# RWKV operands in three DRAM arrays instead of one, in an encoder layer

## The chip, the cores and the metric

The kernel runs on one core of a Trainium2 chip. The time is the device time of one execution in microseconds (us); three runs of the kernel before are given by their median. The core has five engines with an instruction stream each: PE (TensorE, matrix products; its weight loads appear as PEld), DVE (VectorE), ACT (ScalarE), POOL (GpSimd) and SP (SyncE, which here only issues DMA transfers). They meet through semaphores alone. The on-chip memory has 128 partitions, called lanes here.

## The reference, cut to what matters

One encoder layer over 1280 tokens (a prompt of 256 and a sample of 1024): a SwiGLU block, two token mixers side by side (gated linear attention and RWKV-7), cross-attention into 256 memory tokens, and a second SwiGLU block. The change touches the RWKV-7 mixer alone: 8 heads of 64 features, run once forward and once backward in time.

```python
def _rwkv7_scan(r, decay, k, v, kk, a, reverse):
    def step(S, inp):
        r_t, w_t, k_t, v_t, kk_t, a_t = inp
        sa = jnp.einsum('bhij,bhj->bhi', S, -kk_t)
        S = (S * w_t[:, :, None, :] + sa[..., None] * (kk_t * a_t)[:, :, None, :]
             + v_t[..., None] * k_t[:, :, None, :])
        y = jnp.einsum('bhij,bhj->bhi', S, r_t)
        return S, y
...
y = (_rwkv7_scan(rH, dec_f, k2, vH, kk, aH, reverse=False)
     + _rwkv7_scan(rH, dec_b, k2, vH, kk, aH, reverse=True))
```

## The kernel before

The layer is computed in phases that follow one another; each ends when all engines have arrived and the phase's transfers have landed. The two that matter are `rwkv_prepare_phase` and, right behind it, `rwkv_scan_phase`. What passes between them is an array in DRAM, `pack`.

**The preparation** works on four tiles (t = 0 to 3) of 128 lanes by 1280 tokens; a tile holds two heads, lanes 0 to 63 the even one (e = 0) and lanes 64 to 127 the odd one (e = 1). It fills an on-chip tile `rwp_pack` of 128 lanes x 20 chunks x 450 columns: v, r, two runs of accumulated log decay (65 columns for each direction, called g), k, kk and b. ACT copies r (L1200) and v (L1203), DVE writes g (L1258, L1260), k (L1269), kk (L1280) and b (L1282). SP stores the tile in two transfers: first v, r and g (L1126, "store A", semaphore `stored_a`), and when b is there k, kk and b (L1128, "store B", `stored_b`). There is one `rwp_pack` for all four tiles, so in the next tile ACT waits for `stored_a` ahead of its copies, and DVE for `stored_a` ahead of g and for `stored_b` ahead of k. SP's queue is in program order; between the stores stand the loads of the next tile's inputs (L1107), of small weights (L1122), and the stores of gate (L1119) and bonus (L1130). At the phase's end SP waits for every store (L1132).

**The scan** takes 20 steps, one for each chunk of 64 tokens and, at the same time, the backward direction's chunk. It is software-pipelined by hand: a step carries four chunks n, n+1, n+2, n+3 in different stages. For chunk c SP issues eight loads of operands into `rws_pack` (L1379: for each direction and each e two pieces) and eight of v into `rws_hv` and `rws_uv` (L1365); both tiles have two buffers. The loads of chunk c wait until the work of chunk c-2 has read its buffer. ACT's exponentials (L1620, L1621) and POOL's scalings (L1404, L1407, L1417) wait for `loaded`; PE waits for `v_loaded` ahead of `right_side`. A load's DRAM side is made of runs of 64, 129, 192 or 257 floats (256 to 1028 bytes), one for each lane and tile, 256 of them in a transfer.

Of the kernel before, what the change touches and what calls it, by code (L numbers as in the profile page):

```python
# [20 lines left out]
P = 128  # L21
# [13 lines left out]
C = 64  # L35
# [14 lines left out]
V_COL, R_COL, G_COL = 0, C, 2 * C  # L50
K_COL = G_COL + 2 * (C + 1)
KK_COL, B_COL, PACK = K_COL + C, K_COL + 2 * C, K_COL + 3 * C
# [1010 lines left out]
def rwkv_prepare_phase(nc, a, proj_d, pack_d, vecs, bonus_d, gate_d, consts):  # L1063
# [5 lines left out]
    with ExitStack() as ctx:  # L1069
# [13 lines left out]
        stored_a, stored_b, gate_stored, bonus_stored = (m.sem(n) for n in ("stored_a", "stored_b", "gate_stored", "bonus_stored"))  # L1083
        coef, low_scaled, low_ready = m.sem("coef"), m.sem("low_scaled"), m.sem("low_ready")
# [14 lines left out]
        @block.sync  # L1099
        def _(sp):  # L1100
            for j, tile in enumerate((DECAY_TILE, LOW_TILE, GATE_TILE)):
                sp.dma_start(raw2[:, 1, j], proj_d[tile]).then_inc(small_in, 16)
            sp.dma_start(lora[:], a["lora"][0]).then_inc(lora_in, 16)

            def load(t):
                for j, tile in enumerate((R_TILE, KR_TILE, VR_TILE)):
                    sp.dma_start(raw2[:, t % 2, j], proj_d[tile + t]).then_inc(loaded[t % 2], 16)  # L1107

            load(0)
            sp.dma_start(keep[:], a["keep"]).then_inc(keep_in, 16)  # L1110
# [20 lines left out]
            for sem in (stored_a, stored_b, gate_stored, bonus_stored):  # L1131
                sp.wait_ge(sem, 64)  # L1132
# [40 lines left out]
        def _(act):  # L1173
# [7 lines left out]
            for t in range(4):  # L1181
# [32 lines left out]
        def _(dve):  # L1214
            nc.vector.tensor_tensor(stay[:], vecs[:, MU_PREV:MU_PREV + MU_TILES], vecs[:, MU_NEXT:MU_NEXT + MU_TILES], ALU.add).then_inc(coef, 1)
# [19 lines left out]
            for t in range(4):  # L1235
# [8 lines left out]
                for d in range(2):  # L1244
# [7 lines left out]
                    if t:  # L1252
                        dve.wait_ge(stored_a, 16 * t)
                    end = C - 1 if d == 0 else 0
                    first = G_COL + d * (C + 1)
# [11 lines left out]
                if t:  # L1267
                    dve.wait_ge(stored_b, 16 * t)
# [22 lines left out]
def rwkv_scan_phase(nc, pack_d, out, consts):  # L1291
# [8 lines left out]
    with ExitStack() as ctx:  # L1300
# [3 lines left out]
        G_AT, K_AT = C, 2 * C + 2  # L1304
        KK_AT, B_AT, PACKED = K_AT + C, K_AT + 2 * C, K_AT + 3 * C
        pack = slots("pack", [P, 8, PACKED], 2)
# [79 lines left out]
        def _(pool):  # L1386
            for u in range(2):
                nc.gpsimd.memset(pack[u][own(0), :, G_AT + C + 1:G_AT + C + 2], 0.0).then_inc(ready, 1)
                nc.gpsimd.memset(pack[u][own(1), :, G_AT:G_AT + 1], 0.0).then_inc(ready, 1)
            pool.wait_ge(ready, 4)  # L1390
# [3 lines left out]
            pool.wait_ge(ready, 8)  # L1394

            def scale(c):
                packed = lambda at, lanes=slice(0, P): pack[c % 2][lanes, :, at:at + C]
                pool.wait_ge(loaded[c % 2], 128 * (c // 2 + 1))
# [38 lines left out]
        def _(pe):  # L1437
            pe.wait_ge(ready, 8)
# [76 lines left out]
            def step(n, m, p, s):  # L1515
                state, inverting, preparing = n is not None, m is not None, p is not None

                if state:
# [3 lines left out]
                    pe.wait_ge(v_loaded[n % 2], 128 * (n // 2 + 1))  # L1522
# [86 lines left out]
        def _(act):  # L1609
            act.wait_ge(ready, 4)  # L1610

            def exponentials(c):
                act.wait_ge(loaded[c % 2], 128 * (c // 2 + 1))
# [435 lines left out]
def mix_phases(nc, a, proj_d, gla_d, v_d, decay, pack_d, side_d, vecs, mix_o, mix_y, mem, mem_in):  # L2049

    with ExitStack() as mixing:
# [4 lines left out]
        rwkv_prepare_phase(nc, a, proj_d, pack_d, vecs, side_d[0], side_d[1], consts)  # L2056
        rwkv_scan_phase(nc, pack_d, mix_y, consts)
# [3 lines left out]
def build(nc, a, out_d):  # L2061
# [4 lines left out]
    pack_d = nc.dram_tensor("pack", (N_CHUNKS, P, 4, PACK), F32, kind="Internal").ap()  # L2066
# [152 lines left out]
```

## Time and profile before

| | |
|---|---|
| median of 3 runs | 4101.01 us (4097.25 to 4107.3) |
| the profiled execution | 4109.71 us, span 4107.9 us |
| mean granted TensorE clock | 0.942 of full |
| PE, DVE, ACT, POOL busy | 88%, 43%, 26%, 7% of the span |
| preparation (1611 to 1795 us of the span) | 184 us |
| scan (1795 to about 2300 us) | 505 us |

The span runs from the first to the last instruction of one execution; 1.8 us of that execution lie outside. Busy shares are averages over phases with different limits, so the two phases have to be read by themselves.

### The profile page before, as it was taken

The numbers are of one execution on the slowest core, as the hardware profiler recorded it, in microseconds if no ns is written. First come the engines' busy times: TensorE is split into PE (matmuls) and PEld (weight loads), VectorE is DVE, ScalarE is ACT, GpSimd is POOL, SyncE is SP. The second block draws the span as 40 slices with busy tenths as digits, with TensorE's granted clock in tenths as the row PEclk, the third lists the DMA queues.
The fourth block names the chain that finished last, engine by engine and source line by source line (L and its number), as shares of the span: only waits on it lengthen the run. The fifth ranks groups of instructions, "written<-read, shape, count | busy, mean of one in ns | idle before, by whom it ended". The sixth has DMA issues, their size and how long they took to land. (4 is left out here: it accounts for less than half of the span.)

```text
span 4107.9 us, 71757 instructions
## 1 busy us (share of the span) xinstructions
PE 3601.8 (88%) x30856; PEld 3026.3 (74%) x30856; DVE 1753.1 (43%) x2247; ACT 1053.5 (26%) x1355; POOL 303.0 (7%) x295
## 2 busy tenths in 40 slices
PE   7999999997999974548888688797897999999997
PEld 5888888885888873227777466686786888888885
DVE  4545454446121144744444432502235445454445
ACT  2111111104232224435555331312223111111103
POOL 0000000000010010034544100000000000000000
PEclk9999999998999967769999899998999999999998
DMA  2101001000333243663433232001101101011001
GB/s 109 46 31 46 31 32 45 31 21 11 116 123 103 98 127 127 194 147 79 84 78 66 88 105 100 10 31 42 36 21 41 46 31 46 31 39 38 31 21 51
DMA packets 182674, 261.85 MB, mean 64 GB/s; under 512 B 62528, under 2 KB 144832, under 8 KB 176192
## 3 DMA queue, kind: packets, MB, share of 16 engines
q1 hardware_dynamic: 172240, 239.46, 19.3%
q10 hardware_dynamic: 10224, 19.27, 1.2%
q8 instruction: 171, 2.80, 0.3%
q14 instruction: 39, 0.32, 0.0%
HBM read 194.77 MB, written 63.91 MB: 63 GB/s over the span
## 5 line engine op out<-in xcount | busy, mean ns | idle before, releaser
L294 DVE TENSOR_TENSOR main_acc<-main_acc,ffn_psum 128x512 f32<-128x512 f32 (+1 forms) x1056 | 617.5, 598 | 853.8 <-PE ffn_psum L217 852.8
L206 PE MATMUL ffn_psum<-x_xh,ffn_wi_h 128*128 128x512 f32 (+1 forms) x2112 | 525.1, 357 | 49.2 <-DVE ffn_wi_l L283 49.2
L206 PE MATMUL ffn_psum<-x_xh,ffn_wi_l 128*128 128x512 f32 (+1 forms) x2112 | 525.1, 357 | 0.0
L206 PE MATMUL ffn_psum<-x_xl,ffn_wi_h 128*128 128x512 f32 (+1 forms) x2112 | 525.0, 357 | 0.0
L206 PEld LDWEIGHTS ffn_psum<-x_xh,ffn_wi_h 128*128 128x128 f32 x2112 | 372.6, 188 | 117.1 <-DVE ffn_wi_l L283 49.6
L206 PEld LDWEIGHTS ffn_psum<-x_xh,ffn_wi_l 128*128 128x128 f32 x2112 | 349.9, 188 | 60.6
L206 PEld LDWEIGHTS ffn_psum<-x_xl,ffn_wi_h 128*128 128x128 f32 x2112 | 349.3, 188 | 61.1
L217 PE MATMUL ffn_psum<-ffn_hid_h,ffn_wo_h 128*128 128x512 f32 (+1 forms) x1056 | 380.5, 360 | 12.7 <-DVE ffn_hid_l L302 10.0
L217 PE MATMUL ffn_psum<-ffn_hid_h,ffn_wo_l 128*128 128x512 f32 (+1 forms) x1056 | 377.7, 358 | 0.0
L217 PE MATMUL ffn_psum<-ffn_hid_l,ffn_wo_h 128*128 128x512 f32 (+1 forms) x1056 | 376.5, 357 | 0.0
L258 ACT CAST ffn_hid_h<-ffn_hid 128x1280 fp32r<-128x1280 f32 x44 | 55.6, 1264 | 1090.3 <-DVE ffn_hid L300 1090.3
L217 PEld LDWEIGHTS ffn_psum<-ffn_hid_h,ffn_wo_h 128*128 128x128 f32 x1056 | 198.9, 188 | 62.6 <-DVE main_acc L294 12.0
L217 PEld LDWEIGHTS ffn_psum<-ffn_hid_h,ffn_wo_l 128*128 128x128 f32 x1056 | 198.9, 188 | 31.6
L217 PEld LDWEIGHTS ffn_psum<-ffn_hid_l,ffn_wo_h 128*128 128x128 f32 x1056 | 199.3, 189 | 16.7
L677 PE MATMUL mixin_psum<-x_xh,mixin_w_h 128*128 128x512 f32 (+1 forms) x648 | 167.4, 367 | 16.5 <-DVE mixin_w_l L778 16.5
L254 ACT ACTIVATE ffn_hid<-ffn_psum 128x1280 f32<-128x1280 f32 x44 | 54.7, 1243 | 495.2 <-PE ffn_psum L206 495.2
L677 PE MATMUL mixin_psum<-x_xl,mixin_w_h 128*128 128x512 f32 (+1 forms) x648 | 162.5, 359 | 0.0
L677 PE MATMUL mixin_psum<-x_xh,mixin_w_l 128*128 128x512 f32 (+1 forms) x648 | 162.3, 359 | 0.0
L778 DVE TENSOR_TENSOR mixin_w_l<-mixin_w_raw,mixin_w_h 128x1024 fp32r<-128x1024 f32 x27 | 34.5, 1281 | 267.4 <-ACT mixin_w_h L693 267.4
L1441 PE MATMUL rws_psum<-rws_x,rws_gb 64*64 64x64 f32 x3200 | 119.1, 222 | 33.6 <-ACT rws_x L1659 27.7
L1441 PEld LDWEIGHTS rws_psum<-rws_x,rws_gb 64*64 64x64 f32 x3200 | 104.2, 135 | 50.0 <-ACT rws_x L1659 37.7
L677 PEld LDWEIGHTS mixin_psum<-x_xh,mixin_w_h 128*128 128x128 f32 x648 | 109.0, 189 | 39.1 <-DVE mixin_w_l L778 16.9
(279 smaller groups left out, 5391.1 us busy)
## 6 DMA issues: line engine op xcount, KB each, us to landing
ffn_w_raw_in<-ffn_w_in_dram SPq DMA_DIRECT2D x44, 1024.0 KB, 6.3
ffn_w_raw_out<-ffn_w_out_dram SPq DMA_DIRECT2D x44, 512.0 KB, 3.5
mixin_w_raw<-mix_w_in_dram SPq DMA_DIRECT2D x27, 512.0 KB, 3.5
proj<-mixin_stage ACTq DMA_DIRECT2D x18, 640.0 KB, 3.0
pack<-rwp_pack SPq DMA_DIRECT2D x4, 2580.0 KB, 10.7
rws_pack<-pack SPq DMA_DIRECT2D x40, 257.0 KB, 4.5
gla<-main_acc SPq DMA_DIRECT2D x4, 2560.0 KB, 10.1
glas_now<-gla SPq DMA_DIRECT2D x40, 256.0 KB, 3.0
```

Source lines behind the costliest of these rows:

```text
L206: mm = nc.tensor.matmul(ps[:, at + c * BANK:at + c * BANK + tn], w[:, slot, cols], x[:, k, t0:t0 + tn], start=(k == 0 and j == 0), stop=(k ...
L217: mm = nc.tensor.matmul(ps[:, at:at + tn], w[:, slot, o * P:(o + 1) * P], h[:, t0:t0 + tn], start=(j == 0), stop=(j == 2))
L254: nc.scalar.activation(hid[:], ps[:, gate_at:gate_at + T], ACT.Silu).then_inc(silu_done, 1)
L258: nc.scalar.copy(hid_h[:], hid[:]).then_inc(hid_high, 1)
L294: nc.vector.tensor_tensor(acc[:, o, t0:t0 + tn], acc[:, o, t0:t0 + tn], ps[:, at:at + tn], ALU.add).then_inc(added, 1)
L677: mm = nc.tensor.matmul(ps[:, at:at + tn], w[:, u, k * P:(k + 1) * P], x[:, k, t0:t0 + tn], start=(k == 0 and j == 0), stop=(k == KT - 1 a ...
L778: nc.vector.tensor_tensor(w_l[:, u, :], raw[:, u, :], w_h[:, u, :], ALU.subtract).then_inc(split, 1)
L1441: return nc.tensor.matmul(dst, lhs, rhs_, start=start, stop=stop, skip_group_check=True)
```

## The change

The one array becomes three, laid out as the scan reads them: `shared` (r, k, kk, b; chunk, lane, tile, e, 256 columns), `grow` (g, one part for each direction, 66 columns with a zero column that the scan's POOL used to set) and `rwkv_v`. A lane of a chunk is now one run of 8192, 2112 or 2048 bytes, and a load has 64 of them. The scan issues eight transfers a step for sixteen. The preparation's columns are put in another order, and its stores go by halves of the lanes, since the array's rows have 64 lanes: store A is six transfers (v: runs of 256 bytes; g: runs of 264 bytes), store B two (r, k, kk, b: runs of 1024 bytes). As r moves from store A to store B, ACT's copy of r waits for `stored_b` of the tile before instead of `stored_a`.

```diff
@@ rwkv_prepare_phase, SP
-                sp.wait_ge(copied, t + 1)
+                sp.wait_ge(edge_set, 1)
                 sp.wait_ge(v_set, 3 * (t + 1))
                 sp.wait_ge(centred, 4 * (t + 1))
-                sp.dma_start(pack_d[:, :, t, 0:K_COL].rearrange("c p w -> p c w"), pack[:, :, 0:K_COL]).then_inc(stored_a, 16)
+                for e in range(2):
+                    lanes = slice(e * C, (e + 1) * C)
+                    sp.dma_start(v_d[:, :, t, e].rearrange("c l w -> l c w"), pack[lanes, :, V_COL:V_COL + C]).then_inc(stored_a, 16)
+                    for d, (g0, g1) in enumerate(G_ENDS):
+                        sp.dma_start(g_d[d, :, :, t, e].rearrange("c l w -> l c w"), pack[lanes, :, g0:g1]).then_inc(stored_a, 16)
+                sp.wait_ge(copied, t + 1)
                 sp.wait_ge(b_packed, t + 1)
-                sp.dma_start(pack_d[:, :, t, K_COL:PACK].rearrange("c p w -> p c w"), pack[:, :, K_COL:PACK]).then_inc(stored_b, 16)
+                for e in range(2):
+                    lanes = slice(e * C, (e + 1) * C)
+                    sp.dma_start(shared_d[:, :, t, e].rearrange("c l w -> l c w"), pack[lanes, :, R_COL:PACK]).then_inc(stored_b, 16)
@@ rwkv_prepare_phase, ACT
                 if t:
-                    act.wait_ge(stored_a, 16 * t)
+                    act.wait_ge(stored_b, 32 * t)
                 nc.scalar.copy(part(R_COL), view(r[:])).then_inc(copied, 1)
+                if t:
+                    act.wait_ge(stored_a, 96 * t)
@@ rwkv_prepare_phase, DVE
+            nc.vector.memset(pack[:, :, G_COL + C + 1:G_COL + C + 2], 0.0).then_inc(edge_set, 1)
@@ rwkv_scan_phase, SP
                 for d in DIRS:
-                    for e in range(2):
-                        for tile in (hv, uv):
-                            sp.dma_start(tile[c % 2][other(d), d].rearrange("p (q e) t -> p q e t", e=2)[:, :, e],
-                                         pack_d[chunk_of(c)[d]][LANES[e], :, V_COL:V_COL + C]).then_inc(v_loaded[c % 2], 16)
+                    for tile in (hv, uv):
+                        sp.dma_start(tile[c % 2][other(d), d], v_d[chunk_of(c)[d]].rearrange("l q e w -> l (q e) w")).then_inc(v_loaded[c % 2], 16)
...
                 for d in DIRS:
-                    chunk = pack_d[chunk_of(c)[d]]
-                    ends = ((R_COL, G_COL + C + 1), (K_COL, PACK)) if d == 0 else ((R_COL, R_COL + C), (G_COL + C + 1, PACK))
-                    for e in range(2):
-                        dst = pack[c % 2][own(d)].rearrange("p (q e) w -> p q e w", e=2)[:, :, e]
-                        for (s0, s1), at in zip(ends, (0, K_AT if d == 0 else G_AT + 1)):
-                            sp.dma_start(dst[:, :, at:at + s1 - s0], chunk[LANES[e], :, s0:s1]).then_inc(loaded[c % 2], 16)
+                    sp.dma_start(g[c % 2][own(d)], g_d[d, chunk_of(c)[d]].rearrange("l q e w -> l (q e) w")).then_inc(loaded[c % 2], 16)
+                    sp.dma_start(pack[c % 2][own(d)], shared_d[chunk_of(c)[d]].rearrange("l q e w -> l (q e) w")).then_inc(loaded[c % 2], 16)
@@ rwkv_scan_phase, POOL
-            for u in range(2):
-                nc.gpsimd.memset(pack[u][own(0), :, G_AT + C + 1:G_AT + C + 2], 0.0).then_inc(ready, 1)
-                nc.gpsimd.memset(pack[u][own(1), :, G_AT:G_AT + 1], 0.0).then_inc(ready, 1)
-            pool.wait_ge(ready, 4)
```

On SP's queue, one tile of the preparation read as follows before; the shapes are lanes x chunks x columns, and `rwp_pack` is the on-chip tile.

```order
L1126 DMA pack<-rwp_pack 128x20x258 [waits rwp_centred,rwp_v_set,rwp_copied]
L1128 DMA pack<-rwp_pack 128x20x192 [waits rwp_b_packed]
L1130 DMA side<-rwp_bonus 128x1280 [waits rwp_kept]
L1107 DMA rwp_raw<-proj 128x1280 [waits rwp_b_packed]
L1107 DMA rwp_raw<-proj 128x1280 x2
```

It now reads as follows (line numbers are those of the changed file).

```order
L1130 DMA rwkv_v<-rwp_pack 64x20x64 [waits rwp_centred,rwp_v_set,rwp_edge_set]
L1132 DMA grow<-rwp_pack 64x20x66 x2
L1130 DMA rwkv_v<-rwp_pack 64x20x64
L1132 DMA grow<-rwp_pack 64x20x66 x2
L1137 DMA shared<-rwp_pack 64x20x256 [waits rwp_b_packed,rwp_copied]
L1137 DMA shared<-rwp_pack 64x20x256
L1139 DMA side<-rwp_bonus 128x1280 [waits rwp_kept]
```

Two transfers became eight, none moved past another kind; the wait for r's copy stands ahead of store B now.

On SP's queue, the loads of one chunk and one chunk's v in the scan were these.

```order
L1379 DMA rws_pack<-pack 64x4x129 [waits rws_ar_set,rws_bk_set,rws_exps]
L1379 DMA rws_pack<-pack 64x4x192
L1379 DMA rws_pack<-pack 64x4x129
L1379 DMA rws_pack<-pack 64x4x192
L1379 DMA rws_pack<-pack 64x4x64
L1379 DMA rws_pack<-pack 64x4x257
L1379 DMA rws_pack<-pack 64x4x64
L1379 DMA rws_pack<-pack 64x4x257
L1365 DMA rws_hv<-pack 64x4x64
L1365 DMA rws_uv<-pack 64x4x64
```

They are now these.

```order
L1383 DMA rws_g<-grow 64x528 [waits rws_ar_set,rws_bk_set,rws_exps]
L1384 DMA rws_pack<-shared 64x2048
L1383 DMA rws_g<-grow 64x528
L1384 DMA rws_pack<-shared 64x2048
L1375 DMA rws_hv<-rwkv_v 64x512
L1375 DMA rws_uv<-rwkv_v 64x512
```

The order of the loads, and what they wait for, is as it was; each covers 64 lanes before and after.

## Rows read from the trace of the kernel before

**Rows 1.** the page: the span; a DMA queue with its packets, MB, share of 16 engines.

```profile
span 4107.9 us, 71757 instructions
...
q8 instruction: 171, 2.80, 0.3%
```

**Rows 2.** windows: preparation, scan; busy us per engine, PEclk, DMA share, GB/s.

```profile
1611.00:1795.00 184.00, 91.61 (x464) 45.60 (x464) 127.46 (x119) 83.04 (x73) 0.11 (x1) 0.69 0.64 192
...
1854.00:2206.00 352.00, 301.52 (x10572) 268.16 (x10576) 160.70 (x285) 189.02 (x361) 176.14 (x165) 1.00 0.40 79
```

**Rows 3.** who waited for whom, PE, in the scan (1794 to 2300).

```profile
PE rws_psum L1441 <- ACT rws_x L1659: 27.7, 42, 0.7
PE rws_psum L1441 <- issue: 23.6, 32, 2.0
```

**Rows 4.** the same for ACT, then its timeline where that wait ends.

```profile
ACT rws_grown L1620 <- DMA rws_pack<-pack: 24.4, 1, 24.4
...
1804.11 0.65 ACT L1620 ACTIVATE rws_grown<-rws_pack 128x528 f32<-128x528 f32 x1 [24.44 <-DMA rws_pack<-pack]
```

**Rows 5.** timeline of SP's queue: first and last tile of the preparation, scan start.

```profile
1654.66 0.37 SPq L1126 DMA_DIRECT2D pack<-rwp_pack  x1
1669.84 0.37 SPq L1128 DMA_DIRECT2D pack<-rwp_pack  x1
...
1673.50 3.82 SPq L1107 DMA_DIRECT2D rwp_raw<-proj  x3
...
1767.57 0.37 SPq L1126 DMA_DIRECT2D pack<-rwp_pack  x1
1782.75 0.37 SPq L1128 DMA_DIRECT2D pack<-rwp_pack  x1
1784.44 1.77 SPq L1130 DMA_DIRECT2D side<-rwp_bonus  x1
1794.84 1.18 SPq L1379 DMA_DIRECT2D rws_pack<-pack  x2
```

**Rows 6.** waits of SP's queue, end of the preparation.

```profile
SPq L1132 <- DMA side<-rwp_bonus: 5.9, 1, 5.9
```

**Rows 7.** windows of single transfers; the last two columns are DMA share and GB/s.

```profile
1227.00:1231.00 4.00, 4.00 (x23) 3.38 (x22) 0.00 (x0) 0.00 (x0) 0.00 (x0) 1.00 1.04 347
...
1656.00:1660.00 4.00, 3.29 (x4) 1.52 (x5) 1.70 (x2) 1.94 (x2) 0.00 (x0) 0.50 1.04 349
1784.00:1788.00 4.00, 0.00 (x0) 0.00 (x0) 0.41 (x1) 0.00 (x0) 0.00 (x0) 0.69 1.01 325
...
1800.00:1804.00 4.00, 0.00 (x0) 0.00 (x0) 1.27 (x3) 0.00 (x0) 0.00 (x0) 0.50 1.11 204
...
1836.00:1838.00 2.00, 2.00 (x65) 1.78 (x68) 1.42 (x3) 0.52 (x1) 1.27 (x2) 0.82 1.17 151
```

**Rows 8.** timeline of ACT in the second tile, idle time before in brackets.

```profile
1683.82 1.27 ACT L1200 COPY rwp_pack<-rwp_r 128x1280 f32<-128x1280 f32 x1
...
1692.86 1.27 ACT L1206 ACTIVATE rwp_decay<-rwp_kk 128x1280 f32<-128x1280 f32 x1 [6.14 <-DVE rwp_kk L1261]
```

**Rows 9.** timeline of DVE in the same stretch.

```profile
1685.90 1.49 DVE L1258 SCALAR_TENSOR_TENSOR rwp_pack<-rwp_raw 128x1280 f32<-128x1280 f32 x1
...
1693.72 1.49 DVE L1269 TENSOR_TENSOR rwp_pack<-rwp_kr,rwp_raw 128x1280 f32<-128x1280 f32 x1
```

**Rows 10.** DMA issues by line: count, KB each, median us to landing.

```profile
pack<-rwp_pack SPq DMA_DIRECT2D x4, 2580.0 KB, 10.7
...
rwp_raw<-proj SPq DMA_DIRECT2D x15, 640.0 KB, 8.6
...
pack<-rwp_pack SPq DMA_DIRECT2D x4, 1920.0 KB, 12.2
```

**Rows 11.** waits of PE: scan with loads, then its last 83 us.

```profile
PE rws_psum L1441 <- issue: 20.1, 26, 2.0
...
PE rws_psum L1441 <- issue: 1.9, 4, 0.7
```

More of the change, by code:

```diff
@@ L48 @@
 DECAY_UNIT = float(np.exp(-0.5))
-V_COL, R_COL, G_COL = 0, C, 2 * C
-K_COL = G_COL + 2 * (C + 1)
-KK_COL, B_COL, PACK = K_COL + C, K_COL + 2 * C, K_COL + 3 * C
+V_COL, G_COL = 0, C
+R_COL = G_COL + 2 * (C + 1) + 1
+K_COL, KK_COL, B_COL, PACK = R_COL + C, R_COL + 2 * C, R_COL + 3 * C, R_COL + 4 * C
+G_ENDS = ((G_COL, G_COL + C + 2), (G_COL + C + 1, R_COL))
 MEM_T = 512
@@ L1122, in _ @@
                     sp.dma_start(lora[:], a["lora"][t + 1]).then_inc(lora_in, 16)
-                sp.wait_ge(copied, t + 1)
+                sp.wait_ge(edge_set, 1)
                 sp.wait_ge(v_set, 3 * (t + 1))
                 sp.wait_ge(centred, 4 * (t + 1))
-                sp.dma_start(pack_d[:, :, t, 0:K_COL].rearrange("c p w -> p c w"), pack[:, :, 0:K_COL]).then_inc(stored_a, 16)
+                for e in range(2):
[4 more added lines that the diff above has]
+                sp.wait_ge(copied, t + 1)
                 sp.wait_ge(b_packed, t + 1)
-                sp.dma_start(pack_d[:, :, t, K_COL:PACK].rearrange("c p w -> p c w"), pack[:, :, K_COL:PACK]).then_inc(stored_b, 16)
+                for e in range(2):
+                    lanes = slice(e * C, (e + 1) * C)
+                    sp.dma_start(shared_d[:, :, t, e].rearrange("c l w -> l c w"), pack[lanes, :, R_COL:PACK]).then_inc(stored_b, 16)
                 sp.wait_ge(kept, t + 1)
                 sp.dma_start(bonus_d[:, t], bonus[:]).then_inc(bonus_stored, 16)
-            for sem in (stored_a, stored_b, gate_stored, bonus_stored):
-                sp.wait_ge(sem, 64)
+            for sem, each in ((stored_a, 96), (stored_b, 32), (gate_stored, 16), (bonus_stored, 16)):
+                sp.wait_ge(sem, 4 * each)
         @block.tensor
@@ L1252, in _ @@
                     if t:
-                        dve.wait_ge(stored_a, 16 * t)
+                        dve.wait_ge(stored_a, 96 * t)
                     end = C - 1 if d == 0 else 0
-                    first = G_COL + d * (C + 1)
+                    first = G_COL + d * (C + 2)
                     at, edge = (first + 1, first) if d == 0 else (first, first + C)
@@ L1303, in rwkv_scan_phase @@
         HEADS, WIDE = [P, 8, C], [P, 2, 8, C]
-        G_AT, K_AT = C, 2 * C + 2
-        KK_AT, B_AT, PACKED = K_AT + C, K_AT + 2 * C, K_AT + 3 * C
-        pack = slots("pack", [P, 8, PACKED], 2)
+        K_AT, KK_AT, B_AT = C, 2 * C, 3 * C
+        pack, g = slots("pack", [P, 8, 4 * C], 2), slots("g", [P, 8, C + 2], 2)
         decayed, grown, carry = m_.sb("decayed", [P, 8, C + 2]), slots("grown", [P, 8, C + 2], 2), slots("carry", [P, 8, 1], 3)
@@ L1386, in _ @@
         def _(pool):
-            for u in range(2):
-                nc.gpsimd.memset(pack[u][own(0), :, G_AT + C + 1:G_AT + C + 2], 0.0).then_inc(ready, 1)
-                nc.gpsimd.memset(pack[u][own(1), :, G_AT:G_AT + 1], 0.0).then_inc(ready, 1)
-            pool.wait_ge(ready, 4)
             for u in range(4):
                 nc.gpsimd.tensor_copy(ar[u][:, :, 2], each_head(ident)).then_inc(ready, 1)
-            pool.wait_ge(ready, 8)
+            pool.wait_ge(ready, 4)
             def scale(c):
                 packed = lambda at, lanes=slice(0, P): pack[c % 2][lanes, :, at:at + C]
-                pool.wait_ge(loaded[c % 2], 128 * (c // 2 + 1))
+                pool.wait_ge(loaded[c % 2], 64 * (c // 2 + 1))
                 pool.wait_ge(exps, 2 * (c + 1))
@@ L1437, in _ @@
         def _(pe):
-            pe.wait_ge(ready, 8)
+            pe.wait_ge(ready, 4)
             def product(dst, lhs, rhs_, start=True, stop=True):
@@ L1609, in _ @@
         def _(act):
-            act.wait_ge(ready, 4)
             def exponentials(c):
-                act.wait_ge(loaded[c % 2], 128 * (c // 2 + 1))
+                act.wait_ge(loaded[c % 2], 64 * (c // 2 + 1))
                 if c == 1:
@@ L1618, in exponentials @@
                     act.wait_ge(ar_set, 3 * c)
-                g = pack[c % 2][:, :, G_AT:G_AT + C + 2]
-                nc.scalar.activation(grown[c % 2][:], g, ACT.Exp, scale=DECAY_UNIT).then_inc(exps, 1)
-                nc.scalar.activation(decayed[:], g, ACT.Exp, scale=-DECAY_UNIT).then_inc(exps, 1)
+                nc.scalar.activation(grown[c % 2][:], g[c % 2][:], ACT.Exp, scale=DECAY_UNIT).then_inc(exps, 1)
+                nc.scalar.activation(decayed[:], g[c % 2][:], ACT.Exp, scale=-DECAY_UNIT).then_inc(exps, 1)
             def keep_lower(c):
@@ L2055, in mix_phases @@
         gla_finish_phase(nc, proj_d, vecs, mix_o, consts)
-        rwkv_prepare_phase(nc, a, proj_d, pack_d, vecs, side_d[0], side_d[1], consts)
-        rwkv_scan_phase(nc, pack_d, mix_y, consts)
+        rwkv_prepare_phase(nc, a, proj_d, *pack_d, vecs, side_d[0], side_d[1], consts)
+        rwkv_scan_phase(nc, *pack_d, mix_y, consts)
         rwkv_finish_phase(nc, vecs, mix_y, side_d[0], side_d[1], consts, mem, a["mem"], mem_in)
@@ L2065, in build @@
     v_d = nc.dram_tensor("v", (T, 4 * P), F32, kind="Internal").ap()
-    pack_d = nc.dram_tensor("pack", (N_CHUNKS, P, 4, PACK), F32, kind="Internal").ap()
+    pack_d = (nc.dram_tensor("shared", (N_CHUNKS, C, 4, 2, 4 * C), F32, kind="Internal").ap(),
+              nc.dram_tensor("grow", (2, N_CHUNKS, C, 4, 2, C + 2), F32, kind="Internal").ap(),
+              nc.dram_tensor("rwkv_v", (N_CHUNKS, C, 4, 2, C), F32, kind="Internal").ap())
     side_d = nc.dram_tensor("side", (2, P, 4, T), F32, kind="Internal").ap()
```

9 lines of the change are left out of this document (5 added, 4 removed).

## The prediction

> **What bounds the kernel now.** The phases follow one another, so the span of 4107.9 us [rows 1] is a sum, and only the two phases that touch these arrays can move. I read four views. The windows by phase come first: in the preparation (184 us) no engine is full, DVE leads with 127 us and the DMA engines are 0.64 busy; in the scan's main stretch PE is busy for 302 of 352 us while the DMA share is 0.40 [rows 2]. So the scan is PE's chain, with the loads beside it. The waits, second, say the same: the largest things that PE waits for in the scan are ACT's copies (27.7 us) and 23.6 us for which the profile names no releaser ("issue") [rows 3]; no load is in the list, and ACT waits for a load once in the whole scan, for the first one [rows 4]. The reader should see there that the loads of the nineteen later chunks are covered by steps that are longer than they are. Third, SP's timeline shows the preparation's rhythm: store A of the first tile is issued at 1654.66 and of the last at 1767.57, so a tile takes 37.6 us, and store B follows A after 15.2 us [rows 5]. Fourth, the one place where a store is waited for with nothing beside it is the phase's end: SP sits 5.9 us until the last bonus has landed [rows 6], and that bonus stands behind store B in the queue.
>
> **The price of a byte.** Three stretches that hold one kind of transfer each give it [rows 7]. Runs of 1024 bytes stored from all 128 lanes (the `gla` array, at 1227 us) move at 347 GB/s; store A (1656) at 349 and store B (1784) at 325. Loads into 64 lanes, with the DMA engines just as full (share 1.11), move at 204 GB/s (1800), and 256-byte runs into 64 lanes (1836) at 151 GB/s, which is 590 runs a us. No row shows a store from 64 lanes, and none shows runs under 512 bytes written to DRAM: both prices are bounded, not read.
>
> **Store B, at the end.** It grows from 1.97 MB (2560 runs of 768 bytes) to 2.62 MB (2560 of 1024). Before: 1.97 / 0.325 = 6.0 us. After, at the 128-lane rate: 2.62 / 0.347 = 7.6 us, +1.5. After, at the 64-lane rate: 2.62 / 0.204 = 12.8 us, +6.8. The halves stand one behind the other in the queue, so the second doesn't fill what the first leaves idle. I take +6.8: of the two rows, the load into 64 lanes is the one that shares the number of lanes, and nothing but that number sets it apart from the fast ones. Nothing covers this in the last tile, since bonus and the phase's end wait for it. Both ends stay in the range.
>
> The Trainium skill, in SBUF — State Buffer, section "Door 1: The DMA port swizzle", says that 64 consecutive lanes reach only half of the on-chip memory's DMA ports and gives 196 GB/s for them. By that price store B would take 13.4 us and the term would be +7.3; the 204 GB/s of the loads agrees with it, and that it holds for stores too no row here shows.
>
> **Store B, in tiles 0 to 2.** Here it has cover. ACT's copy of r, which now waits for it, starts at 1683.82; after the copies of r and v ACT idles 6.14 us, until 1692.86 [rows 8]. So store B, issued at 1669.84 [rows 5], may land as late as 1683.82 + 6.14 = 1689.96, 20.1 us after its issue, before it costs anything. It landed after 12.2 us in the median [rows 10]; 6.8 us more is 19.0. That fits, by one microsecond: cost 0, and 1 to 4 us a tile if the raw loads behind it (1673.50) slow it further. DVE's k waits for the same store and starts at 1693.72 [rows 9], later still. Late behind the copies of r and v would be store A of the next tile and ACT's square.
>
> **Store A.** Its bytes shrink to 2.01 MB, its runs grow from 2560 to 7680 (2560 of 256 bytes, 5120 of 264). At 349 GB/s it takes 5.8 us, at 590 runs a us 13.0 us. I take 13.0, since the row has the size and the lanes. Of the 3 us by which store A's landing today (10.7 [rows 10]) exceeds 2.64 MB / 0.349 = 7.6, about one may pass before the data move; so it ends some 14 us after its issue, just ahead of store B's issue at +15.2 us [rows 5], so nothing stands behind it; DVE's next write of g, which waits for it, starts at 1685.90 [rows 9], 31 us after the issue. Cost 0, with a thin margin. SP issues six transfers for one, at 0.4 to 0.6 us each; its next work is store B.
>
> **The scan's first loads.** From the first issue (1794.84 [rows 5]) to ACT's first exponential (1804.11 [rows 4]) pass 9.3 us. The chunk's 1.31 MB are the same before and after; at 204 GB/s they are 6.4 us, so issue and landing are 2.9. Eight issues at 0.59 us (two took 1.18 [rows 5]) become four, but the bytes set the end. I take -0.5 us; the ends are 0 and, if long runs moved at 349 GB/s, -2.7.
>
> **The scan's steps.** The later loads are covered by the step (23.3 us: the main stretch moved 27.8 MB [rows 2] at 1.84 MB a step). Eight issues fewer a step are SP's time, for which nobody waits. POOL's four memsets and one DVE memset are under 1 us beside loads. What the loads could touch is PE's idle time without a releaser: 20.1 us in 352 us with all loads, 1.9 in 83 us once only v is loaded [rows 11]. That is 57 against 23 ns per us, so about 34 ns per us, 12 us in all, may come from traffic that delays PE's supply of instructions, which is DMA traffic too (queue q8 [rows 1]). Fewer runs could give all of it back (-12); longer runs could double it (+12). I take 0: 1.84 MB at 204 GB/s is 9.0 us of a 23.3 us step, 0.39, where 0.40 was measured, so the engines stay as full.
>
> **Sum.** +6.8 - 0.5 = +6.3 us. Against the profiled execution (4107.9 us of span and 1.8 around it, 4109.7, which is 8.7 above the median) that is 4116.0; against the median of 4101.0 it is 4107.3.
>
> **The rivals.**
> *Small stores are dear (slower).* If a run of 264 bytes costs twice the 27 ns an engine needs by the row (16 engines, 590 runs a us), store A takes 26 us. The queue then needs 26 + 12.8 and, for a tile's other 3.5 MB (three inputs of 640 KB [rows 10], gate and bonus of the same size, weights), 10 at 0.349, 49 us where a tile has 37.6: 11 us for each of three tiles, of which the slack takes some 4 once, so 29. At the end store B starts 11 us late as well: 4101.0 + 29 + 11 + 6.8 - 0.5 = 4147. It begins to cost at the end from 30 ns a run (14.2 us for 480 runs an engine) and in the tiles from 40 ns. For it: nothing in the profile writes such runs, and the margin is thin. Against it: loads of that size reach 151 GB/s, and store A's 1032-byte runs, which start anywhere, lose nothing against the 1024-byte ones (349 and 347 [rows 7]).
>
> The Trainium skill's page DMA: Bandwidth & Descriptors, section Specifications, puts the least size for full rate at 512 bytes and says that below it the engine reads, modifies and writes. By that rule this rival is the one that comes true.
>
> *The long runs free PE (faster).* The 12 us of idle time go, the first loads gain 2.7 and store B moves at full rate: 4101.0 - 12 - 2.7 + 1.5 = 4088. For it: eight times fewer runs. Against it: the same bytes.
> *The long runs hold PE's instructions up (slower).* An 8192-byte run keeps an engine longer than a 516-byte one; if that doubles the 12 us: 4107.3 + 12 = 4119.
> *It does nothing that counts.* Store B from half the lanes runs like one from all: +1.5 - 0.5, 4102.
>
> **How the numbers follow.** Forecast as summed 0.43, small stores dear 0.21, PE freed 0.12, PE held up 0.12, nothing 0.12. About 12 us (0.3%) is what a measurement of this kernel can tell from no change; "as summed" and "nothing" lie inside, so same 0.55, slower 0.33, faster 0.12. The time is that of the likeliest, 4107, with its own range of 4100 to 4113. For 8 in 10 the range takes in all cases but the dearer half of the small stores and a little of the gain: 4088 to 4130.
>
> **What would show it.** Right: the last wait of SP in the preparation is 11 to 14 us for 5.9; store B alone moves at 190 to 220 GB/s; a tile still takes 37.6 us; the scan's steps are as long as before. Wrong: store A still moving when B is issued, ACT waiting for a store ahead of the copy of r, or PE's time without a releaser far from 24 us. A stage other than these two that changes would mean that I have read the cause wrongly.

## The result: slower by 34 us, most of it in the scan

The changed kernel takes 4143.84 us (median of 7 runs, 4125.53 to 4148.44); the kernel before, run beside it, 4105.03 (7 runs, 4097.25 to 4114.11). The ratio is 1.0083, 95% interval 1.0068 to 1.0098, so 28 to 40 us (the ratio is not that of the medians, which lie 39 us apart). The profiled execution took 4133.71 us. What runs ahead of the two phases, where nothing was changed, was about 7.6 us shorter in it (the first load of the preparation is issued at 1603.79 us, at 1611.44 in the trace of before, and anywhere from 1599.6 to 1617.0 in the thirteen traces of this case), so phases are compared by their own lengths here, not by their place in the span.

The windows of the changed kernel come first: the preparation, a stretch of the scan as long as the one shown before, and the scan from step 1 to step 15. Columns are as in [rows 2].

```profile
1604.00:1795.00 191.00, 90.29 (x464) 46.03 (x464) 127.32 (x119) 83.38 (x73) 0.50 (x1) 0.71 0.77 185
1853.00:2205.00 352.00, 293.72 (x9932) 262.01 (x9932) 152.30 (x268) 177.27 (x338) 160.46 (x154) 0.96 0.31 76
1875.83:2227.90 352.07, 291.97 (x9858) 260.41 (x9860) 150.62 (x266) 176.38 (x336) 160.45 (x154) 0.96 0.32 77
```

The preparation is 191 us for 184, with the same busy times. In 352 us of the scan PE got through 9932 matmuls where it had got through 10572 [rows 2]: 6% less work, some 21 us. The DMA share fell (0.31 for 0.40), and the granted clock, 1.00 before (TensorE's upper level, 2.4 GHz), is 0.96 in the mean.

What PE waited for in the scan of the changed kernel (1794 to 2320), and from step 1 to step 15 alone:

```profile
PE rws_psum L1442 <- issue: 36.4, 28, 2.9
PE rws_psum L1442 <- ACT rws_x L1657: 28.2, 42, 0.7
...
PE rws_psum L1442 <- issue: 32.1, 21, 2.9
```

ACT's copies cost what they did [rows 3]. The time without a releaser went from 23.6 us to 36.4, in fewer and longer pieces. The same stretch of the kernel before, 14 step lengths from ACT's copy of the right side in step 1 to the one in step 15:

```profile
1875.50:2205.17 329.67, 281.30 (x9858) 250.09 (x9860) 149.85 (x266) 175.91 (x336) 163.88 (x154) 1.00 0.41 82
```

It took 329.67 us, with 281.30 us of PE busy and 20.1 us without a releaser; now it is 352.07, 291.97 and 32.1. So +12.0 us of stalls and +10.7 us because the same 9858 matmuls ran longer, less 0.3 us of other waits, make up the +22.4 us. The length of the scan's steps is read from ACT's copy of the right side in step 0 and step 18. The time between them is 443.5 us here and 420.5 before; here are the first exponential and the two copies of the changed kernel, then the two copies of before:

```profile
1803.73 0.64 ACT L1618 ACTIVATE rws_grown<-rws_g 128x528 f32<-128x528 f32 x1 [33.05 <-DMA rws_pack<-shared]
...
1853.43 0.59 ACT L1644 COPY rws_rhs<-rws_psum 128x512 f32<-128x512 f32 x1 [1.27 <-PE rws_psum L1442]
...
2296.96 0.59 ACT L1644 COPY rws_rhs<-rws_psum 128x512 f32<-128x512 f32 x1 [0.36 <-PE rws_psum L1442]
```

```profile
1854.02 0.59 ACT L1646 COPY rws_rhs<-rws_psum 128x512 f32<-128x512 f32 x1 [0.25 <-PE rws_psum L1441]
...
2274.51 0.59 ACT L1646 COPY rws_rhs<-rws_psum 128x512 f32<-128x512 f32 x1 [0.30 <-PE rws_psum L1441]
```

The line of the first exponential answers to [rows 4]. The queue of SP, first and last tile, then the scan's first load, and the wait at the end of the preparation:

```profile
1646.98 0.62 SPq L1130 DMA_DIRECT2D rwkv_v<-rwp_pack  x1
...
1661.66 1.43 SPq L1137 DMA_DIRECT2D shared<-rwp_pack  x2
...
1758.63 0.58 SPq L1130 DMA_DIRECT2D rwkv_v<-rwp_pack  x1
...
1773.81 1.50 SPq L1137 DMA_DIRECT2D shared<-rwp_pack  x2
...
1794.49 0.49 SPq L1383 DMA_DIRECT2D rws_g<-grow  x1
```

```profile
SPq L1141 <- DMA side<-rwp_bonus: 11.2, 1, 11.2
```

A tile takes (1758.63 - 1646.98) / 3 = 37.2 us, 0.4 less than before. From the first load of the preparation to the scan's first load pass 190.7 us for 183.4, +7.3, and the last wait is 11.2 us for 5.9 [rows 6]. The end by itself, from the issue of the last store B to the scan's first load, is 20.7 us for 12.1 [rows 5], +8.6; the three shorter tiles give 1.3 of it back. The first load is 9.24 us ahead of the first exponential, 9.27 before. So the two profiles give +7.3 for the preparation, nothing for the first loads, and +23.0 for the steps: 30 of the 34 us.

Windows of single transfers (store A; store B of the last tile three times; the first loads), to be set beside [rows 7]:

```profile
1651.00:1655.00 4.00, 2.12 (x5) 0.76 (x3) 1.84 (x2) 0.31 (x1) 0.00 (x0) 0.82 0.81 156
...
1776.00:1780.00 4.00, 0.00 (x0) 0.00 (x0) 0.00 (x0) 0.00 (x0) 0.00 (x0) 0.50 0.90 189
1780.00:1784.00 4.00, 0.00 (x0) 0.00 (x0) 0.00 (x0) 0.00 (x0) 0.00 (x0) 0.50 0.92 209
1784.00:1788.00 4.00, 0.00 (x0) 0.00 (x0) 0.00 (x0) 0.00 (x0) 0.00 (x0) 0.50 0.91 188
...
1800.00:1804.00 4.00, 0.00 (x0) 0.00 (x0) 0.97 (x2) 0.27 (x1) 0.00 (x0) 0.50 1.04 226
```

And ACT in the second tile, the copy of r and the square, whose lines before are in [rows 8]:

```profile
1678.44 1.26 ACT L1209 COPY rwp_pack<-rwp_r 128x1280 f32<-128x1280 f32 x1 [1.94 <-DMA shared<-rwp_pack]
...
1684.64 1.27 ACT L1217 ACTIVATE rwp_decay<-rwp_kk 128x1280 f32<-128x1280 f32 x1 [2.86 <-DVE rwp_kk L1273]
```

ACT does wait for store B ahead of the copy of r (1.94 us, in the next tile 2.26), and the idle time ahead of the square shrinks from 6.14 us to 2.86: the cover held. Store A ran later than forecast. SP needed 10 to 12 us to issue its six transfers, and in tiles 0 to 2 its last short runs moved on for 0.6 to 1.1 us after store B had been issued. Between 1661.7 and 1665 us, just behind the first tile's issue of B, these are most of the 77 packets under 512 bytes:

```profile
DMA packets 466, 0.42 MB, mean 126 GB/s; under 512 B 77, under 2 KB 466, under 8 KB 466
```

**One stall, seen closely.** PE's timeline in one step of the changed kernel, then the windows around it:

```profile
1953.01 0.92 PE L1442 MATMUL rws_psum<-rws_ar,rws_bk 64*128 64x192 f32 x8 [0.17 <-ACT rws_rows L1638]
...
1956.66 0.45 PE L1442 MATMUL rws_psum<-rws_ar,rws_hv 64*64 64x64 f32 x7
1959.56 0.64 PE L1442 MATMUL rws_psum<-rws_ar,rws_hv 64*64 64x64 f32 x7 [2.46 <-issue]
1960.14 1.65 PE L1442 MATMUL rws_psum<-rws_ar,rws_bk 64*128 64x192 f32 x8
```

```profile
1950.00:1955.00 5.00, 4.83 (x182) 4.17 (x178) 2.20 (x5) 3.52 (x8) 0.15 (x1) 1.00 0.99 229
1955.00:1960.00 5.00, 2.54 (x83) 2.41 (x76) 0.69 (x1) 2.18 (x5) 4.62 (x6) 0.96 0.31 66
1960.00:1965.00 5.00, 5.00 (x95) 4.33 (x95) 0.76 (x2) 0.79 (x2) 3.82 (x4) 0.50 0.02 3
```

PE stops for 2.46 us in the middle of a run of like matmuls, with the same tiles before and behind the stop, and the view names no releaser: it isn't a load that it lacks. It happens at the end of a burst in which the DMA engines were full (0.99) with the four loads that SP had issued from 1949.14 to 1952.4. After it the granted clock is 0.50, TensorE's lower level (1.2 GHz), in the next 5 us, and the eight matmuls of 64x192 that took 0.92 us before the stall take 1.65. Five microseconds at half the clock are 2.5 us more, so by this estimate the stall cost about 5. Not every stall is followed by a lower clock: behind those of 2.39 us (1982) and 2.95 us (2207) the windows 1985 to 1990 and 2210 to 2215 show 1.00.

What PE lacks there is its instructions, as the packets of 16 KB on queue q8 show, which the profile calls "instruction" (171 packets, 2.80 MB [rows 1]). Three windows of the transfers: 1951.0 to 1951.1 us, 1951.1 to 1956.8, and 1956.8 to 1956.9.

```profile
q8 instruction: 1, 0.02, 60.9%
```

```profile
q1 hardware_dynamic: 243, 1.17, 95.0%
```

```profile
q8 instruction: 1, 0.02, 76.3%
```

One packet of q8 starts at 1951.05 and the next at 1956.83, 5.8 us later, where the median distance from step 1 to step 15 is 4.2; between them the engines move SP's transfers alone. 76.3% of 16 engines in 0.1 us are 1.22 us, so the second packet lands at 1958.05, and PE goes on 1.5 us later. This holds throughout: between 1850 and 2300 us the thirteen traces have 158 PE stalls of over 0.6 us without a releaser, and every one of them ends 1.2 to 1.75 us behind the landing of a q8 packet. A moment taken at random lies there in about one case of seven, and waits with a named releaser end, but for one, anywhere from 0 to 5 us behind a landing.

### The profile page after: what moved, and what is told of

The parts are those of the page before. It is cut to its first block and busy times, and to the rows that moved or that the text cites. A ratio compares the mean times of both kernels' runs of the same rounds, so it can differ in the third digit from the quotient of the medians.

```text
span 4131.9 us, 71625 instructions
## 1 busy us (share of the span) xinstructions
PE 3603.8 (87%) x30856; PEld 3029.4 (73%) x30856; DVE 1754.8 (42%) x2248; ACT 1054.1 (26%) x1355; POOL 297.3 (7%) x291
```

## The experiments

My first theory was the run length: an engine that works on a run of 8192 bytes lets PE's instructions (queue q8 [rows 1]) wait longer than one with runs of 516. The rivals were the size of a transfer and the bytes queued up. Four kernels were made from the changed one:

**e1_pad: the same transfer in runs of 1 KB.** Two unused columns keep the runs apart on the chip.

```diff
-        pack, g = slots("pack", [P, 8, 4 * C], 2), ...
+        pack, g = slots("pack", [P, 8, 4 * C + 2], 2), ...
-  sp.dma_start(pack[c % 2][own(d)], shared_d[chunk_of(c)[d]]...)
+  sp.dma_start(pack[c % 2][own(d), :, 0:4 * C], shared_d[chunk_of(c)[d]]...)
```

> Only the on-chip tile of r, k, kk and b in the scan is padded by two columns a head, so that the same one transfer of 512 KB moves in runs of 1024 bytes for 8192; arrays, stores, number and order of transfers stay. If the length of a run delays PE's supply of instructions (theory), the time without a releaser on PE in the scan falls from 36.4 us to about the 23.6 us of the kernel before, steps 0 to 18 take about 421 us for 443, and the time is some 23 us below the changed kernel, near +10 us against before. If what counts is the share of one transfer that an engine works off at a stretch, or the bytes queued there (rivals), nothing changes: 443 us, some +35 us.

4148.22 us, ratio 1.0086 (1.0054 to 1.0119); steps 0 to 18 450.2 us. Its waits of PE in the scan:

```profile
PE rws_psum L1442 <- issue: 37.7, 21, 3.5
```

Runs an eighth as long, the same stalls: the theory fell. The Trainium skill, in DMA: Bandwidth & Descriptors, section "Queues, rings and completion order", has an engine work off a packet of some 9 to 17 descriptors of one queue before it turns to another. By that rule, if a descriptor is a run, shorter runs would have made shorter waits; this run doesn't show it.

**e2_split: eight transfers of 64 KB**, one for each head, with runs of 1 KB too.

```diff
-  sp.dma_start(pack[c % 2][own(d)], shared_d[chunk_of(c)[d]]...)
+  for j in range(8):
+      sp.dma_start(pack[c % 2][own(d), j], shared_d[chunk_of(c)[d], :, j // 2, j % 2])
```

> The same loads of r, k, kk and b as eight transfers for one, a head each: runs of 1024 bytes and also only 4 KB an engine in one transfer. By run length, as with the padding: about 421 us for steps 0 to 18. By the share of one transfer: 421 us here too, but not with the padding. By bytes queued: 443 us here and there. SP issues 14 transfers a chunk more at 0.6 us, which fits into a step of 23 us.

4109.66 us, ratio 1.0008 (0.9992 to 1.0025); steps 0 to 18 411.2 us, 32 less than in the changed kernel and 9 less than before; clock 1.00 in steps 1 to 15.

```profile
PE rws_psum L1443 <- issue: 13.9, 29, 1.3
```

So cutting the loads takes away the whole loss of the scan. The time is that of before all the same, because the preparation is 8.7 us longer (192.1 for 183.4) and the first exponential comes 13.3 us after the first load for 9.3. How the DMA engines' time is spread shows the difference: the view of the transfers from 1794 to 2300 gives the busy share in 40 slices, in tenths, first of the changed kernel, then of e2_split.

```profile
DMA  8463406060606060606060606060605060510101
...
rws_pack<-shared SPq DMA_DIRECT2D x40, 512.0 KB, 5.9
```

```profile
DMA  3343313141323223141323223242323231011004
...
rws_pack<-shared SPq DMA_DIRECT2D x318, 64.0 KB, 2.7
```

The changed kernel moves in bursts, full and empty by turns; the 18 issues of e2_split, some 0.6 us each, spread the same bytes. The cut thus makes transfers smaller and their issue slower at once; the last experiments below take the two apart.

**e3_paced: each load waits until the one before has landed.**

```diff
   sp.dma_start(g[c % 2][own(d)], ...)
+  sp.wait_ge(loaded[c % 2], 64 * (c // 2) + 32 * d + 16)
   sp.dma_start(pack[c % 2][own(d)], shared_d...)
+  sp.wait_ge(loaded[c % 2], 64 * (c // 2) + 32 * d + 32)
```

> The changed kernel with its 8192-byte runs, but SP waits for each load of a chunk (g and the shared part) to land before it issues the next, so that one load at a time is queued. By queued bytes: PE's time without a releaser falls to 24 us or less, steps 0 to 18 take 421 us or less. By run length or by the share of one transfer: little changes, 440 to 445 us, since each load by itself still puts four runs of 8192 bytes on an engine. The first chunk's loads take longer for everybody: some 6 us more once.

4118.93 us, ratio 1.0024 (1.0007 to 1.0041); 20.6 us without a releaser, the longest still 2.7; steps 0 to 18 423.8 us, and the first exponential 14.5 us after the first load, for 9.3. Keeping the queue short takes away more than half of the stalls that cutting takes away, not all.

**e4_actq: the last tile's second half of store B on ACT's queue.**

```diff
-                for e in range(2):
+                for e in range(2 if t < 3 else 1):
...
+            nc.scalar.dma_start(shared_d[:, :, 3, 1]..., pack[C:P, :, R_COL:PACK])
```

> In the last tile of the preparation alone the second half of store B (lanes 64 to 127) is issued from ACT's queue, so that both halves run at the same time. If half of the lanes reach half of the on-chip memory's rate (theory), the two together move at 325 to 350 GB/s for the 190 of one, and SP's last wait falls from 11.2 to about 6 us. If the new array's layout in DRAM slows the stores (rival), the rate stays near 190 GB/s and the wait at 11 us. The scan stays as in the changed kernel.

One run, 4129.01 us, beside a median of 4107.18 for before. Its transfers in two stretches, by queue (q1 is SP's, q10 ACT's), packets, MB and share of the engines:

```profile
DMA packets 373, 0.38 MB, mean 191 GB/s; under 512 B 0, under 2 KB 373, under 8 KB 373
...
DMA packets 622, 0.64 MB, mean 318 GB/s; under 512 B 0, under 2 KB 622, under 8 KB 622
...
q1 hardware_dynamic: 343, 0.35, 63.9%
q10 hardware_dynamic: 279, 0.29, 39.4%
```

One half alone (1776 to 1778) moves at 191 GB/s; when both are in motion (1780 to 1782) they reach 318. The Trainium skill, in SBUF — State Buffer, section "Can I just issue two DMAs to hit both halves?", gives +6% for that. In this stretch it was +66%; over the whole, from the issue of B to the landing of its later half, 15.5 us for 16.4, it was close to the Trainium skill's 6%. For ACT's half, issued at 1774.30, moved its first packet at 1778.8, so the end came only 2.4 us earlier (from the issue of B to the scan's first load 18.3 us for 20.7). SP's last wait did not fall to 6 us as expected, it is longer:

```profile
SPq L1141 <- DMA shared<-rwp_pack: 13.5, 1, 13.5
```

It also begins earlier, since SP's issue of the bonus took 0.33 us for 5.05. The half lanes are what store B costs; a second queue gives a third of it back.

Next, three kernels for the size of a transfer and for the other way to place the arrays.

**e5_split2: the shared load in two transfers of 256 KB.**

```diff
+  for h in range(2):
+      sp.dma_start(pack[c % 2][own(d), 4 * h:4 * h + 4], shared_d[chunk_of(c)[d], :, 2 * h:2 * h + 2]...)
```

> The changed kernel with the shared load of a step and direction in two transfers of 256 KB (16 KB for each DMA engine, runs of 4 KB) instead of one of 512 KB. Theory, the share of one transfer that an engine works off sets how late PE's instructions come: between the eight-fold split (13.9 us without a releaser, 411.2 us from step 0 to step 18) and the changed kernel (36.4 and 443.5), so about 25 us, 425 to 430 us and a time about 15 us above before, 4115 to 4125. Rival, the bytes queued ahead set it, whatever transfers they are cut into: all 256 KB are queued at once here too, so 36 us, 443 us and some 35 us above before. Rival, what decides is that the queue goes empty between transfers: as the first rival, since two issues leave no gap.

4121.8 us, ratio 1.0039 (1.0025 to 1.0053); steps 0 to 18 429.2 us, both as the theory of the share had them; the 29.0 us without a releaser lie between its 25 and the rivals' 36.

**e6_lanes: the three arrays with 128 lanes by tile**, so that stores leave from all lanes again, and loads of 64 KB.

```diff
-   pack_d = (nc.dram_tensor("shared", (N_CHUNKS, C, 4, 2, 4 * C), ...
+   pack_d = (nc.dram_tensor("shared", (N_CHUNKS, P, 4, 4 * C), ...
-   for e in range(2):
-       sp.dma_start(shared_d[:, :, t, e]..., pack[lanes, :, R_COL:PACK])
+   sp.dma_start(shared_d[:, :, t]..., pack[:, :, R_COL:PACK])
...
+   for j in range(8):
+       sp.dma_start(pack[c % 2][own(d), j], shared_d[chunk_of(c)[d]][LANES[j % 2], j // 2])
```

> The three arrays kept, but as 128 lanes by tile instead of 64 lanes by head: the stores leave all 128 lanes again (four transfers a tile for eight), the shared loads come one for each head (64 KB), the g loads one for each direction and half, the v loads eight a step: 28 loads a step. If the half lanes cost the 7.3 us at the preparation's end and the size of the transfer costs the scan's 23 us: SP's last wait back to 6 to 8 us, preparation 183 to 185 us, steps 0 to 18 about 411 us, time 5 to 10 us below before (4097 to 4102). Rival, the 28 issues of about 0.6 us (17 us a step) bring the loads too late: steps of more than 22 us and a time above before. Rival, the short stores cost more from 128 lanes than from 64: the last wait stays at 11 us.

4100.02 us, ratio 0.9985 (0.9971 to 0.9998). The end of its preparation, PE's stalls, and the first exponential:

```profile
SPq L1137 <- DMA side<-rwp_bonus: 6.7, 1, 6.7
```

```profile
PE rws_psum L1443 <- issue: 11.1, 20, 0.9
```

```profile
1803.78 0.64 ACT L1619 ACTIVATE rws_grown<-rws_g 128x528 f32<-128x528 f32 x1 [30.98 <-DMA rws_pack<-shared]
```

The preparation takes 184.3 us: 6.4 of the 7.3 us are back. Steps 0 to 18 take 409.9 us. What eats half of the gain is the start: the first load was issued at 1789.31, 14.5 us ahead of that exponential, since 20 issues stand in between.

This run also shows what short runs cost by themselves. From all 128 lanes v and g together (runs of 256 and 264 bytes) move at 218 GB/s, g alone at 176, store B (runs of 1024) at 347:

```profile
1650.00:1654.00 4.00, 3.81 (x5) 1.75 (x6) 1.21 (x1) 1.42 (x2) 0.00 (x0) 0.50 0.94 218
1654.00:1658.00 4.00, 0.96 (x3) 0.24 (x2) 2.95 (x2) 1.60 (x2) 0.00 (x0) 0.50 1.23 176
1665.00:1669.00 4.00, 3.94 (x8) 2.03 (x9) 2.48 (x4) 3.98 (x4) 0.00 (x0) 0.68 1.01 347
```

**e7_before_halves: the kernel before, each operand load cut in two.**

```diff
-  sp.dma_start(dst[:, :, at:at + s1 - s0], chunk[LANES[e], :, s0:s1])
+  for q in (slice(0, 2), slice(2, 4)):
+      sp.dma_start(dst[:, q, at:at + s1 - s0], chunk[LANES[e], q, s0:s1])
```

> The kernel before, with each of its eight operand loads of a step cut in two (tiles 0 and 1, tiles 2 and 3), nothing else. Theory, the share of one transfer that an engine works off: halved, so less than the 23.6 us without a releaser, steps 0 to 18 below 420.5 us by 3 to 8 us, time 4098 to 4104. Rival, bytes queued ahead: as before, 23.6 us and 420.5 us, ratio 1.000. Rival, more issues make the loads late: above 420.5 us.

4103.27 us, ratio 0.9989 (0.9977 to 1.0001), on the edge of what can be told. Inside the scan the stalls of [rows 3] fell by more than half, with the runs and bytes of before, and steps 0 to 18 took 413.9 us for 420.5.

```profile
PE rws_psum L1442 <- issue: 9.3, 19, 0.9
```

**e8_first and e9_halves_first: step 0 alone in larger transfers**, of e6_lanes and of e7_before_halves. The edit of the first is shown; the second leaves the loads of step 0 uncut in the same way.

```diff
+  if c == 0:
+      for e in range(2):
+          sp.dma_start(pack[0][own(d)]..., shared_d[chunk_of(0)[d]][LANES[e]])
+      continue
```

> e6_lanes with the loads of step 0 alone in larger transfers: two of 256 KB for each direction in place of eight of 64 KB, so 8 issues for 20 ahead of the first exponential. In e6_lanes the first exponential began 14.5 us after the first load was issued (9.3 in the kernel before); there is hardly any work of PE there that a late instruction could hold up. If the issues set it: 9 to 10.5 us again, the steps as in e6_lanes (about 410 us), time 4 to 5 us below e6_lanes, 4095 to 4098, ratio to before 0.997. Rival, the first step's other waits (the masks and rows that POOL and VectorE prepare) end as late: no gain over e6_lanes.

> e7_before_halves with the loads of step 0 alone uncut, as in the kernel before: the first exponential 12.7 us after the first load in e7_before_halves, 9.3 in the kernel before. If the issues set it: 9 to 10 us, steps about 414 us, time about 3 us below e7_before_halves, ratio to before 0.997 to 0.998. Rival, the first step's other waits end as late: ratio 0.999 as e7_before_halves.

4094.48 us, ratio 0.9966 (0.9954 to 0.9979), and 4093.98 us, ratio 0.9969 (0.9956 to 0.9983). The first exponential came 9.8 and 9.3 us after the first load, 4.7 and 3.4 us sooner than in the kernels they come from; steps 0 to 18 took 413.2 and 413.0 us. Both are faster than the kernel before, by 13 to 14 us; by the profile's parts it would be 7 and 9. The scans repeat what they come from, with 10.7 and 10.0 us without a releaser for 11.1 and 9.3. And the two are equal: the old array with its loads cut in two is worth as much as the three new arrays.

Last, size against pace. A cut transfer is also a slower issue: what falls by cutting may be the share of one transfer or the pile that SP builds up. Two kernels leave the transfers whole and put transfers of 8 bytes, which nothing uses, behind them: one behind each operand load of the kernel before (shown), seven behind each shared load of the changed kernel.

**e10_before_spaced and e11_after_spaced.**

```diff
   sp.dma_start(dst[:, :, at:at + s1 - s0], chunk[LANES[e], :, s0:s1])
+  sp.dma_start(spacer[:, at2:at2 + 2], pack_d[0][0:1, 0, 0:2])
```

> The kernel before with its eight operand loads of a step uncut (up to 16 KB for each DMA engine), and behind each a transfer of 8 bytes that nothing uses: 16 issues of about 0.6 us, as in e7_before_halves, so 1.31 MB are put into the queue in about 10 us (134 GB/s) instead of 4.7 us (278 GB/s). Theory, PE's instructions are late behind bytes that pile up in front of the DMA engines because SP issues faster than they move (204 to 229 GB/s): as in e7_before_halves, 9 to 12 us without a releaser for 23.6, steps 0 to 18 412 to 416 us for 420.5, ratio 0.998 to 0.999. Rival, the share of one transfer that an engine works off counts by itself: 20 to 24 us and about 420 us, as in the kernel before.

> The changed kernel with its shared load in one transfer of 512 KB (32 KB for each DMA engine), and seven transfers of 8 bytes behind each: 18 issues a step, as in e2_split. If only the pace of the issues counts: 12 to 16 us without a releaser, steps 0 to 18 about 411 to 415 us, ratio 1.001 as e2_split. If the 512 KB that one issue puts in front of the engines count by themselves: as in e3_paced, where each load also had the queue to itself, about 20 us and 424 us, ratio 1.003 to 1.005, and a longest stall of over 2 us. If pace does nothing: 36 us, 443 us, 1.008.

In the first the stalls fell from 23.6 us to 15.4 and steps 0 to 18 to 410.9 us in the profiled execution, but the time didn't follow: 4103.33 us, ratio 0.9999 (0.9989 to 1.0009). The profiled execution, 4095.71 us, was the shortest of its ten, so its steps may be shorter than those of the others; and its first exponential came 11.1 us after the first load for 9.3. In the second they fell from 36.4 to 25.9, steps to 428.4 us, ratio 1.0042 (1.0029 to 1.0056).

```profile
PE rws_psum L1447 <- issue: 25.9, 25, 2.4
```

The small transfers were issued faster than I had reckoned (seven in 2.2 us), so the pace was only partly that of the cut kernels. The table sets the scans side by side; "issue time" is what SP took to issue the first chunk's 1.31 MB.

| kernel | largest transfer | issue time | without releaser, longest | steps 0 to 18 | ratio |
|---|---|---|---|---|---|
| changed | 512 KB | 2.5 us | 36.4, 2.9 us | 443.5 us | 1.0083 |
| e1_pad | 512 KB | 2.5 us | 37.7, 3.5 us | 450.2 us | 1.0086 |
| e11_after_spaced | 512 KB | 6.8 us | 25.9, 2.4 us | 428.4 us | 1.0042 |
| e3_paced | 512 KB | by landings | 20.6, 2.7 us | 423.8 us | 1.0024 |
| e5_split2 | 256 KB | 3.7 us | 29.0, 2.8 us | 429.2 us | 1.0039 |
| before | 257 KB | 4.7 us | 23.6, 2.0 us | 420.5 us | 1 |
| e10_before_spaced | 257 KB | 8.4 us | 15.4, 1.4 us | 410.9 us | 0.9999 |
| e7_before_halves | 128.5 KB | 10.4 us | 9.3, 0.9 us | 413.9 us | 0.9989 |
| e2_split | 132 KB (64 for shared) | 11.4 us | 13.9, 1.3 us | 411.2 us | 1.0008 |
| e6_lanes | 66 KB | 12.8 us | 11.1, 0.9 us | 409.9 us | 0.9985 |

In the main the stalls fall with both columns ahead of them. With 512 KB in one transfer a slower pace takes away three to four tenths of the stalls and leaves single ones of over 2 us; with 257 KB and nearly twice the issue time 15.4 us are left, and cut in two 9.3. So neither is the cause alone. The reading that fits all rows is that what counts is how many bytes stand in front of a DMA engine when PE's instructions come to it, be it from one transfer or from several; the traces show when a q8 packet starts and lands, not how long it stood in line. Two profiles of the same scan (the changed kernel and e4_actq) differ by 7 us in the steps (443.5 and 436.9) and by 3 in the stalls (36.4 and 33.1), so one difference of that size says nothing.

## Why the prediction was wrong, point by point

**The step that failed** is the scan's steps: "I take 0: 1.84 MB at 204 GB/s is 9.0 us of a 23.3 us step, 0.39, where 0.40 was measured, so the engines stay as full." They were less full than that (0.32), and it didn't matter, since PE's instructions meet the engines at a moment, not in the mean. Four issues in 2.5 us put 1.31 MB in front of engines that move 204 to 229 GB/s. The stalls cost +12.0 us from step 1 to step 15, the upper bound that I had named; on top of it came the lower clock, +10.7 us in the same stretch, which stood nowhere in the sum.

**The rival that came true** is the one that holds PE's instructions up, given a chance of 0.12 and 4119 us. Its direction was right, and so was what is held up; its reason (the 8192-byte run) was refuted by e1_pad, and its +12 us were half of the 23.0 that the steps lost, because the clock was left out.

**Store B at the end**: +6.8 predicted, +8.6 measured at the end and +7.3 in the whole preparation. In the main it moved at the rate predicted (188 to 209 GB/s for 190 to 220). That the whole preparation fits better is luck: the tiles were 0.4 us shorter each, for which I have no cause. e4_actq shows that the lanes make it, and e6_lanes that all lanes give it back. The argument for the price was weaker than it sounded: the loads at 204 GB/s differ from the fast rows in direction and in their shorter runs as well, not in the lanes alone. The Trainium skill's 196 GB/s for 64 lanes (SBUF — State Buffer, "Door 1: The DMA port swizzle") agrees with these stores too.

**Store B in tiles 0 to 2, and store A**: right, cost 0, though all three signs of being wrong came true. ACT waited for the store, but 2 us of a slack of 6, and the tile took 37.2 us. Store A was still moving when B was issued in tiles 0 to 2, since its six issues took 10 to 12 us and not the 0.4 to 0.6 each that I had put; the slack took that in. Only the third sign, PE's time without a releaser, cost anything. Store A moved at 156 GB/s, which at a mean of 262 bytes is 595 runs a us, for the 590 assumed.

**Small stores are dear**, the largest rival at 0.21: it didn't happen, since a run cost what the sum had for it and not twice that. Short runs are slow, as that price already said; e6_lanes shows it from all lanes (176 and 218 GB/s for 347). The Trainium skill's rule that full rate needs 512 bytes (DMA: Bandwidth & Descriptors, Specifications) agrees with these rates; I was wrong to conclude from it that the rival's doubled price would come true.

**The first loads**: -0.5 predicted, 0 measured.

The range ended at 4130 because the chance that the loads do harm was held small and its price was capped at a doubling of the stalls alone. Against the +6.3 us of the sum stand 34 measured: +7.3 of store B, +23.0 of the steps, and some 4 that the parts of one profiled execution don't show.

What stays open: whether the shorter steps of e10_before_spaced are those of one short execution, and whether the clock falls because of the stalls alone. In the rows it falls behind some of them and not behind others of the same length, and it stayed at 1.00 from step 1 to step 15 of e2_split and e6_lanes; no run tried it by itself.

## What to carry to other kernels

Fewer and larger transfers save the issuing queue's time, which is worth something only where somebody waits for that queue; where a full engine streams instructions, a burst of large loads in its shadow can cost more than it saves, though no wait names a load. Look at the time without a releaser, its longest piece, the packets of the instruction queue that land just ahead of its end, and the DMA share in slices of a step instead of the mean, and cut or space the loads until the slices are even; where nothing else runs yet, as at a phase's start, leave them large. And when a layout is changed for the reader, look at what it does to the writer's lanes.

## What the runs showed that I had not expected

In the scan, all 158 stalls of PE of over 0.6 us without a releaser end 1.2 to 1.75 us behind the landing of a 16 KB packet of q8. The granted clock fell to 0.50 for 5 us right behind a PE stall of 2.46 us; eight matmuls of 64x192 took 1.65 us there for 0.92. Two stores from opposite halves of the lanes, on two queues, moved at 318 GB/s together for 2 us, 191 alone. Seven transfers of 8 bytes in a row were issued every 0.32 us; those of 64 KB take 0.6. And the kernel before had 14 us of such stalls to give (23.6 to 9.3 us) without a change of its layout, which with step 0 left large were worth 13 us of its time.
